# Layer 1 of a two-layer trunk: high and rest activations as one 512-column operand, the two halves of each bank added by VectorE

## The reference

```python
for layer in range(2):
    p = split_columns(modulate(rms_norm(x, norm1[layer]), sh1, sc1) @ w_in[layer])   # and for ctx
    y_m = mlstm_bidirectional(...)        # 4 heads, gated by p[3]
    y_a = latent_attention(...)           # 8 heads, keys of context and latent tokens
    y_c = gate_b * short_conv(gate_c * u) # cb * conv3(cc * cu)
    merged = (sigmoid(ga) * (y_m @ w_pm) + sigmoid(gb) * (y_a @ w_pa) + sigmoid(gc) * (y_c @ w_pc))
    x = x + g1 * merged @ w_o
    x = x + g2 * square(relu(modulate(rms_norm(x, norm2[layer]), sh2, sc2) @ w_up)) @ w_down
    # ctx is updated in the same way, in layer 0 only
return rms_norm(x, final_norm)
```

## Time and profile before

| | us |
|---|---|
| median of 3 runs | 1948.4 (1947.9 to 1950.4) |
| profiled execution, its time | 1943.7 |
| its span, first to last instruction | 1941.9 |
| TensorE busy | 1872.9, 96% |
| VectorE busy | 979.1, 50% |
| ScalarE busy | 689.9, 36% |
| GpSimd busy | 729.6, 38% |
| mean granted TensorE clock | 0.986 |

### The profile page before, as it was taken

One profiled execution on the slowest core, in us unless ns is written; L12 is line 12 of the kernel. 1 busy time (PEld: TensorE's weight loads), 2 busy tenths in 40 slices (PEclk: granted clock), 3 DMA queues, 4 the chain that ended last, 5 costly groups with the idle time before them and its releaser, 6 DMA issues.

```text
span 1941.9 us, 27168 instructions
## 1 busy us (share of the span) xinstructions
PE 1872.9 (96%) x11175; PEld 1607.7 (83%) x11175; DVE 979.1 (50%) x1372; ACT 689.9 (36%) x946; POOL 729.6 (38%) x513
## 2 busy tenths in 40 slices
PE   5999899999999999999999999999999999979998
PEld 3697688778878788778877778799997999969997
DVE  4454543645433443366443544644657656547554
ACT  3333532433222232243232222433543444434443
POOL 2332231112543344544222322432332566746553
PEclk7999999999999999999999999999999999989999
DMA  9221122122444334465225337222232355565562
GB/s 315 66 88 44 44 66 73 58 65 66 150 132 130 111 127 147 135 197 169 91 90 184 107 118 240 81 94 88 66 122 97 109 181 189 174 195 173 177 191 91
DMA packets 240858, 244.64 MB, mean 126 GB/s; under 512 B 6020, under 2 KB 239840, under 8 KB 240736
## 3 DMA queue, kind: packets, MB, share of 16 engines
q1 hardware_dynamic: 240432, 242.80, 39.5%
q10 hardware_dynamic: 304, 0.10, 0.0%
HBM read 241.83 MB, written 1.05 MB: 125 GB/s over the span
## 4 chain that ended last, share of the span: by engine, by line
PE 89%; DVE 4%; SPq 2%; issue 1%; ACT 1%; DMA 1%; POOL 1%; DVEq 0%; ACTq 0%; POOLq 0%
PE pp L931 19%; PE pp L935 19%; PE pp L932 19%; PE pp L939 4%; PE pp L938 4%; PE pp L940 4%; PE pc L1099 3%; PE pp L913 2%; PE pp L915 2%; PE pp L914 2%; SPq L827 2%; PE pc L1020 2%; PE pc L1151 1%; PE pc L1189 1%; DVE wL L1605 1%
## 5 line engine op out<-in xcount | busy, mean ns | idle before, releaser
L1492 POOL TENSOR_TENSOR wL<-raw,wH 128x512 fp32r<-128x512 f32 x360 | 580.2, 1632 | 854.4 <-ACT wH L1203 854.3
L931 PE MATMUL pp<-hH,wH 128*128 128x512 f32 (+1 forms) x1760 | 590.5, 346 | 19.3 <-ACT hH L1388 14.3
L1605 DVE TENSOR_TENSOR wL<-raw,wH 128x512 fp32r<-128x512 f32 x360 | 459.2, 1299 | 266.4 <-ACT wH L1203 261.0
L932 PE MATMUL pp<-hH,wL 128*128 128x512 f32 (+1 forms) x1760 | 582.1, 341 | 0.0
L1203 ACT ACTIVATE wH<-raw 128x1024 fp32r<-128x1024 f32 x360 | 360.3, 1049 | 336.0 <-PE pp L940 222.1
L935 PE MATMUL pp<-hL,wH 128*128 128x512 f32 (+1 forms) x1760 | 457.2, 341 | 2.6 <-POOL hL L1543 1.7
L931 PEld LDWEIGHTS pp<-hH,wH 128*128 128x128 f32 x1760 | 335.6, 191 | 66.8 <-issue 17.8
L932 PEld LDWEIGHTS pp<-hH,wL 128*128 128x128 f32 x1760 | 336.0, 191 | 37.1 <-issue 1.0
L935 PEld LDWEIGHTS pp<-hL,wH 128*128 128x128 f32 x1760 | 304.7, 191 | 44.2 <-POOL hL L1543 6.6
L938 PE MATMUL pp<-yH,wH 128*128 128x512 f32 (+1 forms) x448 | 150.6, 336 | 0.0
L939 PE MATMUL pp<-yL,wH 128*128 128x512 f32 (+1 forms) x448 | 150.6, 336 | 0.0
(11 more groups left out here) (228 smaller groups left out, 2097.3 us busy)
## 6 DMA issues: line engine op xcount, KB each, us to landing
raw<-in_w_in SPq DMA_DIRECT2D x84, 1024.0 KB, 5.2
raw<-in_w_up SPq DMA_DIRECT2D x32, 1024.0 KB, 5.6
raw<-in_w_down SPq DMA_DIRECT2D x32, 1024.0 KB, 5.2
ada_T<-in_w_ada SPq DMA_DIRECT2D x18, 1024.0 KB, 7.9
ada_G<-in_w_ada SPq DMA_DIRECT2D x12, 1024.0 KB, 8.5
ada_Y<-in_w_ada SPq DMA_DIRECT2D x10, 1024.0 KB, 13.0
ada_H<-in_w_ada SPq DMA_DIRECT2D x8, 1024.0 KB, 9.2
raw<-in_w_proj_m SPq DMA_DIRECT2D x8, 1024.0 KB, 5.2
```

The source lines that it names most:

```text
L931: pe.matmul(dsts[b], wh[b], hi[:, kt, ts_], start=first, stop=False)
L932: pe.matmul(dsts[b], wl[b], hi[:, kt, ts_], start=False, stop=False)
L1492: pool.tensor_tensor(wL[:, p % RAW, ks, :], raw[:, p % RAW, ks, :], wH[:, p % HIGH, ks, :].bitcast(F32), ALU.subtract).then_inc(wL_ready, 1)
L1605: dve.tensor_tensor(wL[:, p % RAW, ks, :], raw[:, p % RAW, ks, :], wH[:, p % HIGH, ks, :].bitcast(F32), ALU.subtract).then_inc(wLv_ready, 1)
```

## The change

The tiles hH and hL become the two halves of one tile hHL, and yH and yL of yHL, at the same addresses. For the layer-1 panels other than mk, ak, mv and av (`folded`), the high activation's products go to columns 0 to 255 of the bank and the rest activation's product to columns 256 to 511. Where the loop has no wait, L938 and L939 become one matmul whose moving operand is high and rest side by side, 2 x 256 columns, with one weight load. In the branch that waits, there are three matmuls as before, the third with the other half of the bank as its output. VectorE then adds the two halves with a reduction into `fold`, the context half of gs, frees the slot, and signals `fold_ready`; the readers read `fold` in SBUF in place of `pp` and count `fold_used`, for which the next reduction waits. Cut to its core:

```diff
-        hH = at("hH", [P, KT, TOK], F32R, o); o += K16
-        hL = at("hL", [P, KT, TOK], F32R, o); o += K16
+        hHL = at("hHL", [P, 2, KT, TOK], F32R, o); o += 2 * K16
+        hH, hL = hHL[:, 0], hHL[:, 1]
...
-        yH = at("yH", [P, KT, TOK], F32R, o); o += K16
-        yL = at("yL", [P, KT, TOK], F32R, o); o += K16
+        yHL = at("yHL", [P, 2, KT, TOK], F32R, o); o += 2 * K16
+        yH, yL = yHL[:, 0], yHL[:, 1]
...
         gs = at("gs", [P, NB, TOK], F32, o); o += NB * TOK * 4
+        fold = gs[:, :, 0:CTX]
...
+        def folded(st):
+
+            return st["l"] == DEPTH - 1 and st["kind"] not in ("mk", "ak", "mv", "av")
+
+        fold_no = {st["p"]: i for i, st in enumerate(q for q in PANELS if folded(q))}
+
+        def result(st):
+
+            return fold if folded(st) else pp[:, st["p"] % 2, :, slice(0, TOK) if st["kind"] in ("mk", "ak") else cols(st["l"])]
+
+        def result_ready(eng, st):
+
+            p = st["p"]
+            if folded(st):
+                eng.wait_ge(fold_ready, fold_no[p] + 1)
+            else:
+                eng.wait_ge(panel_done, p + 1)
+
+        def result_used(eng, st):
+
+            eng.sem_inc(fold_used if folded(st) else slot_free[st["p"] % 2], 1)
...
                 hi, lo, ready, need = operand(st)
+                both = hHL if ready is h_ready else yHL
...
-                    dsts = [pp[:, slot, b, ts_] for b in range(NB)]
+                    dsts = [pp[:, slot, b, slice(0, LAT) if folded(st) else ts_] for b in range(NB)]
+                    rests = [pp[:, slot, b, LAT:TOK] for b in range(NB)] if folded(st) else dsts
...
                         for b in range(NB):
-                            last = pe.matmul(dsts[b], wh[b], lo[:, kt, ts_], start=False, stop=end)
+                            last = pe.matmul(rests[b], wh[b], lo[:, kt, ts_], start=False, stop=end)
+                        continue
+                    if folded(st):
+                        for b in range(NB):
+                            pe.matmul(pp[:, slot, b, :].rearrange("p (x t) -> p x t", x=2), wh[b], both[:, :, kt, ts_],
+                                      start=first, stop=False)
+                            last = pe.matmul(dsts[b], wl[b], hi[:, kt, ts_], start=False, stop=end)
                         continue
...
                     ts_ = cols(l)
-                    src = pp[:, slot, :, ts_]
+                    src = result(st)
+                    if folded(st):
+                        n = fold_no[p]
+                        dve.wait_ge(panel_done, p + 1)
+                        if n:
+                            dve.wait_ge(fold_used, n)
+                        dve.reduce_sum(fold, pp[:, slot, :, :].rearrange("p b (x t) -> p b t x", x=2), AX).then_inc(fold_ready, 1)
+                        dve.wait_ge(fold_ready, n + 1)
+                        dve.sem_inc(slot_free[slot], 1)
...
                     elif kind == "proj":
-                        dve.wait_ge(panel_done, p + 1)
+                        result_ready(dve, st)
...
-                        dve.sem_inc(slot_free[slot], 1)
+                        result_used(dve, st)
...
-                                i = dve.scalar_tensor_tensor(out=xT[:, kt, hs], in0=pp[:, slot, b, hs],
+                                i = dve.scalar_tensor_tensor(out=xT[:, kt, hs], in0=fold[:, b] if folded(st) else pp[:, slot, b, hs],
                                                              scalar=modT[:, l, g + kt, v:v + 1], in1=xT[:, kt, hs],
```

More of the change, by code:

```diff
@@ L586, in trunk @@
         panel_done = sem("panel_done")
+        fold_ready = sem("panel_halves_added")
+        fold_used = sem("added_halves_used")
         slot_free = [sem(f"slot_free{i}") for i in range(2)]
@@ L1242, in _ @@
                     ts_ = slice(0, TOK) if kind in ("mk", "ak") else cols(l)
-                    src = pp[:, slot, :, ts_]
+                    src = result(st)
                     if kind in ("mk", "mq"):
-                        act.wait_ge(panel_done, p + 1)
+                        result_ready(act, st)
                         w = 1 if kind == "mk" else 0
@@ L1249, in _ @@
                         act.wait_ge(mqk_ready, 4 * l + (c_ + 1 if w else 3 + c_))
-                        act.sem_inc(slot_free[slot], 1)
+                        result_used(act, st)
                     elif kind == "mo":
-                        act.wait_ge(panel_done, p + 1)
+                        result_ready(act, st)
                         act.activation(sig_o[:, c_ % 2, :, ts_], src, ACT.Tanh, scale=0.5).then_inc(so_exp, 1)
                         act.wait_ge(so_exp, l * MH + c_ + 1)
-                        act.sem_inc(slot_free[slot], 1)
+                        result_used(act, st)
                     elif kind in ("ak", "aq"):
@@ L1702, in _ @@
                         for b in range(NB):
-                            i = dve.tensor_tensor(y_tmp[:, b, ts_], pp[:, slot, b, ts_],
+                            i = dve.tensor_tensor(y_tmp[:, b, ts_], src[:, b],
                                                   c_acc[:, b, sg, :].rearrange("p s t -> p (s t)"), ALU.mult)
```

11 lines of the change are left out of this document (5 added, 6 removed).

## The result

| | before | after |
|---|---|---|
| median of the runs of this comparison | 1949.41 us (4 runs) | 1984.34 us (4 runs, 1983.68 to 1987.82) |
| ratio to before, 95% interval | | 1.0181, 1.0165 to 1.0197 |
| profiled execution: time, span | 1943.7, 1941.9 us | 1983.8, 1982.0 us |

The change costs 35 us by the medians and 40.0 by the two profiled executions; the forecast was 1980. First the busy time of the page, then the stages of layer 1 and of its attention, and then the group of the new instruction with the waits of TensorE (line; what it waited for: us in total, times, longest).

What follows compares the result with a forecast made beforehand. TensorE, 96% busy, was taken as the bound, delayed by VectorE's serial chains. Added waits of 35.3 us less 3.5 for joins gave +31.8, 1975.5 from the profiled execution; plus 4.7 to the median, 1980 us, range 1957 to 1998.

Steps and rivals of the forecast that it cites:

- What is joined: Layer-1 matmuls: 256 pairs become one matmul where the code skips the waiting branch; 832 other pairs stay separate.
- Rival (e): The change joins everywhere: 1088 pairs save 14.7 us instead of 3.5, giving 1969 us; chance 0.01.
- What a join saves: On TensorE, from the pitches of 256- and 512-column matmuls: 0.0135 us a join, 3.5 us for 256.
- What the addition costs: On VectorE, one reduction for each of 82 layer-1 panels: 1.23 us, 1.27 with semaphore, 104 us in all.
- Rival (b): Every reduction takes 1.76 us, 0.53 longer: +57 us, giving 2005 us; chance 0.07.
- Contention in the update: xT update reading both operands in SBUF while GpSimd subtracts there: may wait up to 1.1 us.
- up panels: VectorE's turn grows to about 6.7 us against 5.76; TensorE waits 3.1 us per group in down, 12.4 in all.
- Convolution: Panels cc, cu, cb: VectorE slips 2.75 us per triple, banks are freed late, TensorE stalls 6 us; gate/proj behind recover.
- wo and norm: Additions of wo 2 and 3 delay the mean, 2.5 us; the first up's delays the row copy, 1.3: 3.8.
- Attention: Additions delay the prT copy 0.7 us beside a gate, 1.3 beside a proj, 2 at the first gate: 9.3.
- End: After TensorE is done, ScalarE waits for the xT update: one addition longer, 1.3 us.
- rival (c): Longer waits bring one dip of TensorE's granted clock in each of the later seven attention heads: +12, 1992 us; chance 0.10.

Runs made afterwards that it cites:

- experiment 3: Changed kernel without additions or products of the rests, 1232 pairs joined, 688 with the operand in one piece: 1936.78 us, ratio 0.9945 to the kernel before.
- experiment 11: Changed kernel with wo and down joined but not added up, xT updated in two steps straight from PSUM: 1984.20 us, ratio 1.0189 to the kernel before.
- experiment 6: Changed kernel with only the 16 up panels back in their old form, without addition: 1973.72 us, ratio 1.0143 to the kernel before.
- experiment 7: Changed kernel with only the first of the bank's two blocks added up in up panels, the second left out: 1979.89 us in one run.
- experiment 8: Changed kernel with every addition of the up panels done twice: 2011.84 us in one run.
- Experiment 9: Changed kernel with only the 12 convolution panels cc, cu, cb back in their old form: 1976.22 us, ratio 1.0151 to the kernel before.
- experiment 1: Changed kernel with its 256 joins but no addition, the product of the rests left out: 1944.03 us, ratio 0.9983 to the kernel before.
- experiment 2: Changed kernel without additions or products of the rests, with 1232 pairs joined: 1938.43 us, ratio 0.9952 to the kernel before.
- experiment 12: Kernel with whole result, 384 joins, additions only in gate/proj 1 and aq, each without the last panel: 1946.37 us, ratio 0.9990 to the kernel before.
- experiment 10: Changed kernel with aq and the gate and proj panels of branch 0 back in their old form: 1978.71 us, ratio 1.0164 to the kernel before.

## Why the prediction was right, and where it was not

The direction, the range and the likeliest case held: 1984.3 for 1980, in 1957 to 1998. The mechanism held too, additions on VectorE that reach TensorE through serial chains, with the largest terms in up and in the attention; several terms of the sum did not.

- **What is joined.** Right: 256 pairs (L966 x224 on yHL, the rest on hHL), TensorE's count down by 256. The number of pairs that are not joined was wrong, without effect on the sum: 82 panels have 1312 pairs, so they are 1056, the 832 on h and wo and 224 more of proj and down in the branch that waits. Rival (e) would have been 17.7 us of joins, not 14.7.
- **What a join saves.** Mis-sized: 6.6 ns for 13.5, 1.7 us for 3.5. The step took the pitch of 512 columns from a row of 512-column matmuls alone. In the new order they alternate with matmuls of 256 columns, and there it is 0.235. My lower bound named the two-piece operand as the danger; experiment 3 shows that it isn't that.
- **What the addition costs.** Right: 1215 ns for 1.23 us. Rival (b) is out.
- **Contention in the update.** Right in kind: 1284 ns in the median for 476. GpSimd as the cause is backed by experiment 11 as far as this: with one operand in PSUM the slowing is gone. The rule that I quoted from the Trainium skill (SBUF — State Buffer, Who interferes with whom) agrees with it, and with the reduction, 1209 to 1225 ns over all 82; that one reads PSUM here, so its being a reduction was not tested. The price falls only where GpSimd works in SBUF at that moment: of the 40 updates, the 22 that run beside a subtraction of GpSimd take 1190 to 1514 ns, the 18 others 473 to 489; c_u and y_tmp, which also read the sum from SBUF, meet none and stayed between 418 and 428 ns. One such meeting reaches the path, the product of the last proj:

```profile
L1709 DVE SCALAR_TENSOR_TENSOR gs<-gs x8: 691/692/1558, 1561.2 to 1722.8; 128x512 f32<-128x512 f32 x8
```

  GpSimd, which adds this product to the merged rows, was free at 1723.83 us and began at 1724.47: 0.6 us of the wait in wo below.
- **up panels.** Forecast 3.1 us a group, measured 1.8 at most. The turn was right, 6.56 to 6.59 us for 6.64. Wrong was "I let about 1 us of lateness stay at the start of a group": VectorE reaches the group on time. These are VectorE's rows, one turn in the third group:

```profile
1876.29 1.22 DVE L1695 TENSOR_REDUCE gs<-pp 128x512 f32<-128x1024 f32 x1
1878.22 0.69 DVE L1754 TENSOR_TENSOR y_tmp<-y_tmp 128x512 f32<-128x512 f32 x1 [0.70 <-ACT y_tmp L1333]
1879.61 0.69 DVE L1758 TENSOR_TENSOR yHL<-y_tmp,yHL 128x512 fp32r<-128x512 f32 x1 [0.70 <-ACT yHL L1241]
1880.56 0.69 DVE L1638 TENSOR_TENSOR wL<-raw,wH 128x512 fp32r<-128x512 f32 x1 [0.26 <-ACT wH L1236]
1881.50 1.45 DVE L1638 TENSOR_TENSOR wL<-raw,wH 128x512 fp32r<-128x512 f32 x1 [0.26 <-ACT wH L1236]
1882.88 1.21 DVE L1695 TENSOR_REDUCE gs<-pp 128x512 f32<-128x1024 f32 x1
```

  No row waits for TensorE: each idle time is a hand-over to ScalarE and back, a serial chain longer than the 5.76 us of a panel. Three turns of 0.8 us excess and the last addition of 1.27 are 3.7 us, to which the 2.0 until yH is there come; TensorE arrives there at 4.3, so it waits 1.4, and measured were 1.5 in the three later groups, 1.8 in the first. That the stage still lost 11.2 of the forecast 12.4 is for the greater part the clock of the first group, 3.4 us by the estimate; 0.8 is the longer wait of the ada turn (L1064), which the forecast has under wo and norm. Experiments 6 to 8 show the threshold.
- **Convolution.** Forecast 6 of waits for a freed bank, measured 4.7 of wait (DVEq L1697) plus 1.7 of clock. The waits began in the third triple, not the second, and 1.4 of the 4.7 lie behind the convolution, at the first proj and the second gate of the third branch. Then "the gate/proj panels behind it have room to recover" failed. VectorE's additions there start 11.13 us apart for two panels, of 11.52 that TensorE takes:

```profile
1702.82 1.21 DVE L1695 TENSOR_REDUCE gs<-pp 128x512 f32<-128x1024 f32 x1
...
1713.95 1.21 DVE L1695 TENSOR_REDUCE gs<-pp 128x512 f32<-128x1024 f32 x1
```

  At 0.4 us a pair the lateness of the convolution can't be made good, and it reaches the merged rows: TensorE waits 4.2 us for them in the first wo panel, which the forecast put at nothing. Experiment 9 shows where it came from.
- **wo and norm.** Forecast 3.8, lost 6.2 together with the above, at most 2.0 of it clock. It is not more because the last wo panel had a wait of its own, 4.3 us before and 1.6 now. The table of waits names DVEq L1739 for it, but VectorE had nothing to do then; ScalarE, which splits this panel's weights, waited for the transfer. Its rows before and after:

```profile
1716.24 2.00 ACT L1203 ACTIVATE wH<-raw 128x1024 fp32r<-128x1024 f32 x2 [12.11 <-DMA raw<-in_w_out]
```
```profile
1739.01 2.01 ACT L1236 ACTIVATE wH<-raw 128x1024 fp32r<-128x1024 f32 x2 [10.72 <-DMA raw<-in_w_out]
```

  Lateness that arrives ahead of a wait for a transfer takes its place in part.
- **mLSTM and q/k.** Forecast 2.5, lost 3.5: 0.9 beside the mo panels, 2.6 at the last two aq, of which up to 1.7 is clock.
- **Attention.** Forecast 9.3, measured 9.8, of it 8.6 as the growth of the wait for prT, as named. The parts differ. From the third head on, where the clock is full, the waits are 1.05 us beside a gate and 2.03 beside a proj:

```profile
1488.98 1.95 PE L1184 MATMUL pc<-k_a,q_a 128*128 128x512 f32 x4 [1.05 <-DVE prT L2045]
...
1501.25 1.96 PE L1184 MATMUL pc<-k_a,q_a 128*128 128x512 f32 x4 [2.03 <-DVE prT L2045]
```

  That is 0.6 and 1.5 more than before, where the forecast had 0.7 and 1.3. But only three proj panels lie ahead of such a copy, not four, and the first gate cost 1.4, not 2. The longest wait, 2.8 at the first proj, lies above "1.1 to 1.7"; only one addition stands ahead of its copy, and why it is longer than the others stays open. The half-clock stretches at 1462 and 1475.7 us lie beside it.
- **End.** Forecast 1.3, measured 2.5: there are two such places. Before the last panel TensorE turns rows of the output, and that wait (L1036 for f_x) also grew by one addition, from 1.2 to 2.6 us in total.
- **The clock, rival (c).** I gave it as a case of its own, with a dip in each head. It came as part of every case: 8.6 us by the estimate, in the attention less than feared (1.5), more in the up stage. Without it the losses are 30.2 where my terms gave 31.8.
- **Luck.** The sum came near partly because waits forecast too high (up, by some 5 us) covered one forecast at nothing (4.2 in the first wo panel) and savings that were half as large. Between the two profiled executions the kernel lost 40.0 us, 8 more than the sum; between the medians it lost 35. I had added 4.7 us to get from the profiled execution before, a quick one, to its median; after, the profiled execution was only 0.6 under its median. So the forecast of the time is nearer than that of the loss in the trace that it was made from.

## What to carry to other kernels

An engine with half its time free can still be the bound: compare its serial chain for one unit of work, hand-overs included, with the time that the other engine takes for the unit. While the chain stays below that time, added work is free. Above it the excess adds up from unit to unit, and what it costs is the part that exceeds the slack before the next consumer: in the up panels 4.3 us until down needs the last result, which half an addition, with turns of 6.03 us for 5.76, did not use up. Lateness is carried along until a stage with real slack, which a stage at 11.13 of 11.52 us is not. And measure the price of an operation in the order in which it will stand: a saving of 13.5 ns taken from uniform rows was 6.6 in alternation.

## What the runs showed that I had not expected

- A 512-column matmul that alternates with 256-column ones starts the next 0.235 us later, in a row of its like 0.227; the layout of its operand in one or two pieces changes nothing that shows.
- Idle time of TensorE is paid twice, at least in part. In the changed kernel it works 32.8 us at half clock from the start of layer 1 to the end, 15.7 before. In the traces with no addition or few (before and experiments 1, 2, 3 and 12) it is 14 to 23 us, in the nine others, the changed kernel among them, 25 to 56. With doubled additions, every later group of up and down gained a stretch at half clock of 6.8 us. Such stretches also come and go where nothing differs: the v panels have none, one of 3.4 or one of 6.8 us, in different executions. So a gain seen where it was made need not be in the total of one execution, as in experiments 10 and 11.
